# Attention split by engine and interleaved over both streams, with four modulation bursts moved to the output projection

## What is computed

```python
sm, cm, gm, sf, cf, gf = modulation(c, mod_w[l], mod_b[l])        # silu(c) @ w_mod, 2048 x 12288
h = rms_norm(x, norm_mix_pre[l]) * (1 + cm) + sm
q_a, k_a, v_a, q_b, k_b, v_b, u_c, v_c = split_projection(h, w_in[l])   # 2048 x 4608; gelu on u_c, v_c
o_a = neighbourhood_attention(...)    # 6 heads; context stream: plain attention
o_b = window_attention(...)           # 6 heads on 2 key heads, rotary, sink logit
o_c = chunk_gmlp(u_c, v_c, ...)       # layer norm, 128 x 128 mixing, gating
x = x + gm * rms_norm(merge_heads(o_a, o_b, o_c, w_out[l]), norm_mix_post[l])   # 2048 x 2048
x = ffn_sublayer(x, sf, cf, gf, ...)  # 5632 wide SwiGLU
```

## Time and profile before

| | us |
|---|---|
| median of 3 runs (2419.17 to 2423.46) | 2419.4 |
| the profiled execution | 2421.94 |
| its span | 2420.2 |
| TensorE busy | 2294.1 |
| VectorE busy | 1624.5 |
| ScalarE busy | 994.1 |

### The profile page before, as it was taken

The page is one execution under the profiler, slowest core; times in us unless marked ns, Lnnn a source line. Parts: engine busy times, 40 slices in busy tenths (PEclk is TensorE's granted clock), DMA queues, the critical chain, the costliest instruction groups (busy, mean ns, idle before and its releaser), DMA issues.

```text
span 2420.2 us, 27975 instructions
## 1 busy us (share of the span) xinstructions
PE 2294.1 (95%) x10686; PEld 1804.9 (75%) x10686; DVE 1624.5 (67%) x1738; ACT 994.1 (41%) x1284; POOL 68.9 (3%) x97
## 2 busy tenths in 40 slices
PE   5999878999999999999999998799999999999998
PEld 2776545778878888788777886487888888878886
DVE  2555443469988889888887996446888644454455
ACT  2333232364444444334346344346444444433443
POOL 1000010000000000000000101000000000000000
PEclk8999988999999999999999999899999999999999
DMA  8779888858878878788875897665877666656664
GB/s 305 271 278 340 331 291 304 297 178 296 285 258 291 289 264 295 249 275 286 287 244 204 306 316 245 230 184 169 278 269 254 211 195 190 186 178 195 190 219 148
DMA packets 269317, 609.91 MB, mean 252 GB/s; under 512 B 19116, under 2 KB 19296, under 8 KB 267840
## 3 DMA queue, kind: packets, MB, share of 16 engines
q1 hardware_dynamic: 264832, 589.37, 71.8%
q0 software_dynamic: 4352, 18.76, 2.1%
HBM read 603.79 MB, written 5.45 MB: 252 GB/s over the span
## 4 chain that ended last, share of the span: by engine, by line
PE 84%; DMA 7%; DVE 5%; issue 2%; ACT 2%; POOL 1%; SPq 0%; POOLq 0%; DVEq 0%; ACTq 0%
PE bank_A L849 39%; PE bank_B L849 38%; DMA mraw<-in_mod_w 6%; PE bank_M L909 2%; PE bank_X L937 2%; DVE wlo L1448 1%; PE bank_M L898 1%; ACT whi L1157 1%; PE bank_T L929 1%; DMA raw<-in_w_in 0%; DMA raw<-in_w_gate 0%; ACT junk L1171 0%; PE bank_M L838 0%; DVE xt_lo L1497 0%; POOL rstd L707 0%
## 5 line engine op out<-in xcount | busy, mean ns | idle before, releaser
L1448 DVE TENSOR_TENSOR wlo<-raw,whi 128x1024 fp32r<-128x1024 f32 x724 | 880.1, 1222 | 611.1 <-ACT whi L1157 610.5
L1157 ACT CAST whi<-raw 128x1024 fp32r<-128x1024 f32 x724 | 758.9, 1050 | 1178.0 <-PE bank_A L849 579.3
L849 PE MATMUL bank_B<-whi,xt_lo 128*128 128x512 f32 x1104 | 433.3, 392 | 1.1 <-DVE wlo L1448 0.6
L849 PE MATMUL bank_A<-whi,xt_lo 128*128 128x512 f32 x1088 | 429.6, 395 | 4.2 <-DVE xt_lo L1497 3.7
L849 PE MATMUL bank_B<-wlo,xt_hi 128*128 128x512 f32 x1104 | 429.9, 389 | 0.0
L849 PE MATMUL bank_B<-whi,xt_hi 128*128 128x512 f32 x1104 | 429.7, 389 | 0.0
L849 PE MATMUL bank_A<-wlo,xt_hi 128*128 128x512 f32 x1088 | 426.0, 392 | 0.0
L849 PE MATMUL bank_A<-whi,xt_hi 128*128 128x512 f32 x1088 | 425.7, 391 | 0.0
L1469 DVE SCALAR_TENSOR_TENSOR acc<-mraw,cond,acc 128x1024 f32<-128x1024 f32 x300 | 371.0, 1278 | 0.0
L849 PEld LDWEIGHTS bank_A<-whi,xt_lo 128*128 128x128 f32 x1088 | 205.9, 189 | 64.0 <-issue 19.8
L849 PEld LDWEIGHTS bank_B<-whi,xt_lo 128*128 128x128 f32 x1104 | 207.2, 188 | 54.9 <-issue 11.9
(11 more groups left out here) (231 smaller groups left out, 1623.6 us busy)
## 6 DMA issues: line engine op xcount, KB each, us to landing
mraw<-in_mod_w SPq DMA_DIRECT2D x384, 512.0 KB, 5.6
raw<-in_w_gate SPq DMA_DIRECT2D x176, 512.0 KB, 4.4
raw<-in_w_up SPq DMA_DIRECT2D x176, 512.0 KB, 4.4
raw<-in_w_down SPq DMA_DIRECT2D x176, 512.0 KB, 4.9
raw<-in_w_in SPq DMA_DIRECT2D x144, 512.0 KB, 5.4
raw<-in_w_out SPq DMA_DIRECT2D x64, 512.0 KB, 4.8
gate_mix<-gate_rows POOLq DMA_DIRECT2D x4, 1024.0 KB, 6.8
gate_ffn<-gate_rows POOLq DMA_DIRECT2D x4, 1024.0 KB, 9.4
```

The source lines that it names most:

```text
L849: mm = pe.matmul(bank[f"{pair}{s}"][:], xs[:, k, t], w[:, kb, :], start=(k == first and n == 0), stop=(k == (nk - 1 if last is None else l ...
L1157: act.copy(weights(u * UNIT + ph)[0], raw[:, ph % RING]).then_inc(hi_ready, 1)
L1448: dve.tensor_tensor(lo, raw[:, ph % RING], hi.bitcast(F32), ALU.subtract).then_inc(lo_ready, 1)
```

## The change

- The step list is the same for both layers and finer: `score` is cut into `score` (PE), `top` (DVE) and `exp` (ACT); `value` into `turn_p`, `mix` and `keep`; `gate_c` into `gate_c` and `lift`; `turn_c` into `turn_c` and `keep_c`. The steps of both streams and groups are interleaved. Waiting for z is a step of PE (`z`), both gelus stand near the front, the cached keys are transposed before the first score.
- Seven bursts stay in each attention. The second half of their last chunk goes behind piece 2 of the projection in both layers; layer 0's projection also has bursts behind pieces 5, 8, 11, 13, 16, 19, 21 and 24. SP issues their weights behind pieces 3 and 4 later in SP's own order. Tails go with them (`OUT_ENDS`).
- `ln_b` is kept in `junk` instead of a part of `pt`. POOL does its two powers for the layer norm ahead of `gate_store`. The output projection waits for each part of its input where it reads it first.

```diff
-MOD_OUT = [ND // 2, 0]
+MOD_OUT = [ND, 0]
...
+OUT_MODS = [{2: (-1, range(4, 8))}, {2: (-1, range(4, 8))}]
+OUT_MODS[0].update({q: (h // 2, range(4 * (h % 2), 4 * (h % 2) + 4)) for h, q in enumerate((5, 8, 11, 13, 16, 19, 21, 24))})
+OUT_FETCH = [{q + 3 + h: (mi, js[2 * h:2 * h + 2]) for q, (mi, js) in mods.items() if mi >= 0 for h in range(2)}
+             for mods in OUT_MODS]
+OUT_ENDS = [{2: -1, 24: ND - 1}, {2: -1}]
...
+def attention_steps():
...
+    first, second = ("mod_first",), ("mod_second",)
+    s = [first, ("z",), ("gelu", 0), ("turn", 0, 1), ("turn", 0, 3), ("turn", 0, 0), ("turn", 0, 2), ("turn", 0, 4), ("gelu", 1)]
+    s += [("turn_ck", 0), ("turn_ck", 1), ("score", 0), second, ("top", 0), ("exp", 0), ("bias",), ("sinks",), ("turn", 1, 2)]
+    s += [("turn_ws",), ("score", 1), ("top", 1), ("turn", 1, 4), ("turn", 1, 1), ("turn", 1, 3), ("exp", 1), ("soft", 0)]
+    s += [("turn", 1, 0), ("turn_p", 0), first, ("soft", 1), ("mix", 0), ("norm_v", 0), ("keep", 0), ("turn_p", 1)]
+    s += [("score", 2), ("top", 2), second, ("mix", 1), ("keep", 1), ("exp", 2), ("score", 3), ("top", 3), ("soft", 2)]
+    s += [("gate_c", 0), ("exp", 3), ("gate",), first, ("lift", 0), ("turn_p", 2), ("mix", 2), ("norm_v", 1), ("soft", 3)]
+    s += [second, ("turn_p", 3), ("turn_c", 0), ("keep", 2), ("keep_c", 0), ("gate_c", 1), ("mix", 3), ("lift", 1)]
+    s += [("turn_c", 1), first, ("keep", 3), ("keep_c", 1)]
+    return s
...
-        crossed, ln_b = pt[:, 0:8, :], pt[:, 8:12, :].rearrange("p t c -> p (t c)")
+        crossed, ln_b = pt[:, 0:8, :], junk[:]
...
                     if step[0] == "mod_first":
-                        mod_chunk(m_att, l, range(UNIT // 2 if l == 0 and m_att == m - 1 else UNIT))
+                        mod_chunk(m_att, l)
...
-                gate_store(l, 0)
                 for s in range(2):
                     power(vmv[:, s, 1:2], vrstd[:, s:s + 1], vmv_ready, 2 * l + s + 1, vrstd_ready)
+                gate_store(l, 0)
...
-                for step, banks in got.items():
-                    if step[0] in ("value", "turn_c"):
-                        for b, i in banks[-2:]:
-                            read(b, i)
+                mixed = {0: [("mix", 0), ("mix", 2)], NH: [("mix", 1), ("mix", 3)], 2 * NH: [("turn_c", 0), ("turn_c", 1)]}
...
+                        if i == 0 and k in mixed:
+                            for step in mixed[k]:
+                                for b, n in got[step]:
+                                    read(b, n)
...
+                    for j in range(UNIT - (i == ND - 1)):
+                        ahead(split, u + i, j, 1)
+                        if i * UNIT + j in OUT_ENDS[l]:
+                            mod_row(m + OUT_ENDS[l][i * UNIT + j])
```

More of the change, by code:

```diff
@@ L166, in mod_ends @@
+BANKS_OF = {"top": "score", "exp": "score", "keep": "mix", "lift": "gate_c", "keep_c": "turn_c"}
 def mod_ends(m):
@@ L287, in attention @@
                 banks = [self.turn()]
+            elif step[0] == "turn_p":
+                banks = [self.turn() for _ in range(2 if step[1] < 2 else 3)]
             elif step[0] == "score":
                 banks = [self.acc() for _ in score_banks(step[1])]
-            elif step[0] == "value":
-                banks = [self.turn() for _ in range(2 if step[1] < 2 else 3)] + [self.acc() for _ in range(2)]
+            elif step[0] == "mix":
+                banks = [self.acc() for _ in range(2)]
             elif step[0] == "gate_c":
@@ L1019, in attention @@
                             mm.then_inc(filled[b], 1)
-                    elif kind == "value":
+                    elif kind == "turn_p":
+                        n = step[1]
+                        pe.wait_ge(pn_ready, 4 * l + n + 1)
+                        blocks = [prob[:, n % 2, h, w * P:(w + 1) * P] for h in range(NH) for w in range(1 + n // 2)]
+                        for j, (b, i) in enumerate(banks):
+                            turn(b, i, blocks[4 * j:4 * j + 4])
+                    elif kind == "mix":
                         n = step[1]
                         s, ty = divmod(n, 2)
[L1023 to L1028, removed]
+                        for b, i in got[("turn_p", n)]:
                             read(b, i)
-                        for (b, i), heads in zip(outs, (range(0, 4), range(4, 6))):
+                        for (b, i), heads in zip(banks, (range(0, 4), range(4, 6))):
                             free(b, i)
@@ L1300, in attention @@
                     kind = step[0]
-                    if step in GELU_BEFORE:
-                        s = GELU_BEFORE.index(step)
+                    if kind == "gelu":
+                        s = step[1]
                         act.activation(z[:, s, U_C:W_IN], z[:, s, U_C:W_IN], ACT.Gelu_apprx_tanh).then_inc(gelu_ready, 1)
-                    if kind == "mod_second" and m < plan.at[(l, "out")][1] + MOD_OUT[l] - 1:
-                        mod_row(m)
                     elif kind in ("turn", "turn_ck", "turn_ws"):
@@ L1762, in attention @@
                         dve.tensor_tensor(v, v, ln_b, ALU.add).then_inc(vn_ready, 1)
-                    elif kind == "gate_c":
+                    elif kind == "lift":
                         s = step[1]
@@ L1772, in attention @@
                         ins.then_inc(freed[b], 1)
-                    elif kind == "turn_c":
+                    elif kind == "keep_c":
                         s = step[1]
```

125 lines of the change are left out of this document (49 added, 76 removed).

## The result

The changed kernel takes 2396.8 us (median of 4 executions, 2389.3 to 2398.6) against 2420.1 (4 executions, 2419.2 to 2423.5): 0.989 of the time, 95% interval 0.988 to 0.991, which is 23 us less. Two more sets of four gave 2390.4 and 2391.5 (first experiment). The direction and the range held; the three medians lie 10 to 17 us above the 2380 forecast.

The account below looks back on a forecast made before the run. TensorE, 95% busy, bounds the kernel; its attention waits come from the mraw ring (layer 0) and mainly the softmax chain (layer 1). -23.1 - 28.5 + 7.6 + 3 + 1.9 = -39.1 us from 2419.4 gives 2380; 80% between 2366 and 2402.

Parts of the forecast that it names:

- Attention, layer 1: Layer 1's attention stage: each turn costs a turn of the mraw ring, -23.1 us, bounds -28 and -15.
- the walk: Hand walk through layer 1's new attention list, each engine in order: mraw ring ends last, stage end moves 1572.4 to 1549.3.
- B: Rival for both attention stages: the softmax chain paces them, layer 1 saves 11.4 us, layer 0 25; 2395 us, chance 0.18.
- Attention, layer 0: Layer 0's attention stage: seven bursts paced by the mraw ring end at 380.5, not 408.98; -28.5 us, bounds -34 and -20.
- part (5): ln_b to junk, GpSimd's powers ahead of gate_store, gates behind the last score: costed at nothing, covered by the first output chunk.
- Output projection, layer 0: Layer 0's output projection: four more bursts cost +7.6 us, DMA stalls at two short gaps +3, bounds 0 and 12.
- wrong altogether: Sign of failure: attention over 75 us in either layer, or more than 12 us of waits in the projection.
- the turn of 6.2 us: Layer 0's quickest mraw turn, set against two-piece gaps of 5.44 us in its projection; 1.5 us stall taken for each.
- A: The forecast for both attention stages: the mraw ring paces them, 7 turns each; 2380 us, chance 0.50.
- Rival C: Layer 0's projection starves: weights arrive at 330 GB/s, +12 us for +3, 2389 us; at 283 GB/s 2405; chance 0.15.
- Output projection, layer 1: Layer 1's output projection: one more burst without DMA pressure, +1.9 us, bounds 1.8 and 3.
- My 377 GB/s over 85 us: Layer 0's projection: 61 transfers, 32 MB, pass on average at this rate in 84.9 us, with +3 us of stalls.

Follow-up runs that it names:

- first experiment: The changed kernel repeated without an edit, as the yardstick for the others: 2390.4 us, ratio 0.9865, in its first repeat and 2391.5 us, ratio 0.9875, in its second.
- Experiment 4: Against the changed kernel, modulation pieces that SP asks for in attention were fetched by half, 256 KB, with the same matmuls and waits: 2376.4 us, ratio 0.9806.
- experiment 3: The old order of steps, with seven bursts in each attention and the changed kernel's projections: 2423.8 us, ratio 1.0013 against the kernel before.
- experiment 7: The even kernel with the gate's rows loaded earlier, so that their 2 MB travel inside attention: 2391.8 us, ratio 0.9866.
- even kernel: The changed kernel with all nine bursts of layer 0's output projection three pieces apart, behind pieces 1, 4, 7, ... 25: 2381.4 us, ratio 0.9834, and 2381.0, ratio 0.9843.

## Why the prediction was right in direction and 10 to 17 us short

**Attention, layer 1: right, by its mechanism.** Predicted -23.1, measured -24.6. Experiment 4 shows that the ring held the stage and not the softmax chain, but the lead is smaller than in the walk: the first, third and sixth of the six turns ended by the chain of work, where the walk had that for the first, with a tie at the fifth. So B's mark came for half of the turns, but not its price of 11.4 us saved: with half pieces the new order goes through the stage in 51.6 us, where the old order with seven bursts takes 75.0 (experiment 3). From the first burst's end (1483.1) to the seventh's (1538.7) are 55.6 us; the walk had 57.0. That the sum came so near is partly luck, since two sizes were off and nearly cancel: the turn beside the stores took 11.5 us for 9 (its leg 9.76), the one where I had the gate's rows 8.3 for 12.

**Attention, layer 0: right mechanism, somewhat more.** Predicted -28.5 with an outer bound of -34, measured -35.0. The 12 us turn beside the gate's rows didn't come (8.6 us from 367.1 to 375.7), and the turn of 9.8 beside the stores was 8.4. Here part (5) failed: I put the rows' transfer in the last turn of attention and costed their new place at nothing, with the first output chunk as cover for their *use*. Their *bytes* have no such cover. They are not among the 61 transfers of my sum for the projection, and they met the first `w_out` pieces (10.37 us leg), the splits, and with them a tail that waits 1.3 us for VectorE in layer 0 and 1.5 in layer 1. Whether the projection pays for them is not shown: its first two bursts wait 0.75 and 1.7 us, but experiment 7, which sends the rows earlier, left it at 117.4 us, between the even kernel's two. Beside the ring the turn there is 12.2 and 13.5 us.

**Output projection, layer 0: the failed step.** Predicted +7.6 for four bursts and +3 of stalls; measured +25.4. The floor is as predicted: four bursts at 1.92 and a tail of 0.8 are 8.5. The other 16.9 us, against a bound of 12 in the prediction, are 12.0 of waits (the two rows of waits above) and 4.9 of matmuls that ran longer, at the lower clock shown below (busy time grew by 13.4 us, from 100.3 to 113.7, of which 8.5 are the floor). My own sign for "wrong altogether", more than 12 us of waits in the projection, was reached or passed in two of the three profiles of this kernel: 12.0, 12.7 in the first repeat and 9.8 in the second. The step that was wrong is the turn of 6.2 us, taken from attention's quickest leg of 4.59, at the two gaps of two pieces. The chain at the first of them:

```profile
421.93 1.06 ACT whi L1155
...
423.01 1.24 DVE wlo L1444
424.25 0.74 SPq L560
...
425.04 0.47 SPq L554
...
425.55 8.79 DMA mraw<-in_mod_w
...
434.48 1.93 PE bank_M L906 x8
```

The burst behind piece 11 ends at 423.6. SP, in its own order, first asks for a `w_out` piece (424.25), which must wait for the split of 423.01, and only then for the last piece of modulation weights (425.04); that one is 8.79 us under way between `w_out` traffic, and the burst behind piece 13 ends at 436.41. The turn is 12.7 us where the products and the burst itself cover 7.4. Its second like, and what follows either:

```profile
436.41 6.21 PE bank_B L846 x24
...
459.20 9.06 DMA mraw<-in_mod_w
...
470.32 6.34 PE bank_A L846 x24
```

The two gaps cost 5.2 and 4.6 us rather than 1.5 each (7.1 and 6.5 from the end of the products to that of the burst, less 1.92; 1 us of it is the second half of a burst at the lower clock), and the two pieces behind them took 6.21 and 6.34 rather than 5.44. The gaps of three pieces cost little once the queue is in step, 1.7 us behind piece 5 and 0.75 behind piece 2. Experiment 5, in which the two short gaps are gone, brought 9.0 and 10.4 us back, about what the two gaps cost. That the bursts are also spread over two more pieces there was not separated.

**Luck in the sum.** Layer 0's attention (-35.0, bound -34) and its projection (+25.4, where the bounds gave at most +19.6) both lay outside what I had allowed, in opposite directions. They cancel in part, and as far as that goes the nearness of the total is luck. The total by itself would even have pointed at B, which had 2395: only the stage times tell A from B.

**Rival C came nearer in size, not in kind.** At 330 GB/s it gave 2389, and the sets measured 2390 to 2397. But its mark was a DMA share of 1.0 throughout; the changed kernel has 0.86 at 309 GB/s, with stretches of idle queues between the stalls. The limit it names appears in the even kernel, whose windows stand below.

**The lower clock was not in the sum at all.** In the term for layer 0's projection I took every matmul behind the start at full speed, because the earlier trace rows show 0.98 where TensorE never waits. With waits in it that doesn't hold. Ten-us windows of the changed kernel (columns as in the earlier trace rows):

```profile
425.00:435.00 10.00, 5.92 (x32) 3.68 (x34) 2.45 (x2) 2.09 (x2) 0.00 (x0) 0.96 0.93 347
435.00:445.00 10.00, 10.00 (x44) 7.12 (x36) 2.43 (x3) 3.30 (x6) 0.00 (x0) 0.87 0.94 351
445.00:455.00 10.00, 10.00 (x52) 6.91 (x51) 4.69 (x6) 3.21 (x4) 0.00 (x0) 1.00 0.78 271
...
465.00:475.00 10.00, 6.61 (x26) 4.11 (x27) 1.23 (x1) 2.01 (x2) 0.00 (x0) 0.83 1.03 407
475.00:485.00 10.00, 10.00 (x57) 7.01 (x56) 4.97 (x5) 4.73 (x9) 0.00 (x0) 1.00 0.69 234
```

The window of its first repeat with the lowest clock:

```profile
440.00:450.00 10.00, 7.46 (x25) 4.74 (x26) 1.23 (x1) 1.33 (x2) 0.00 (x0) 0.66 1.03 409
```

Windows of the even kernel's second profile:

```profile
375.30:385.00 9.70, 7.11 (x40) 4.78 (x40) 0.00 (x0) 0.00 (x0) 0.00 (x0) 1.00 1.01 411
385.00:395.00 10.00, 9.97 (x52) 7.50 (x44) 4.99 (x5) 4.68 (x5) 0.00 (x0) 1.00 1.04 414
395.00:405.00 10.00, 10.00 (x53) 6.89 (x51) 3.40 (x4) 3.14 (x3) 0.00 (x0) 1.00 1.01 361
...
425.00:435.00 10.00, 9.59 (x50) 6.33 (x49) 3.67 (x3) 2.29 (x4) 0.00 (x0) 1.00 0.99 343
435.00:445.00 10.00, 9.02 (x47) 5.81 (x46) 3.99 (x5) 4.36 (x7) 0.00 (x0) 1.00 0.99 348
```

In the changed kernel the windows that hold the end of a long wait, or the one after it, show a granted clock of 0.83 to 0.96; in the first repeat one shows 0.66, so the larger part of it ran at 1.2 of the 2.4 GHz. In the even kernel's second profile, with at most 1.4 us waited at once, all ten-us windows of the stage stand at 1.00; in its first, the window behind waits of 2.9 and 1.3 us shows 0.70. The length of a wait alone doesn't decide it: in the second repeat of the changed kernel, waits of 0.9 and 1.4 us at the start of the stage went with this window:

```profile
385.00:395.00 10.00, 8.11 (x35) 5.91 (x36) 5.00 (x5) 4.58 (x5) 0.00 (x0) 0.83 0.79 260
```

**Output projection, layer 1: right**, +2.2 for +1.9.

**Rates.** The Trainium skill (DMA: Bandwidth & Descriptors, section Where 436 GB/s comes from) has about 358 GB/s per core as the HBM's side. Here ten-us windows of the even kernel's projection start reach 411 and 414 GB/s; five in a row behind them, from 395 to 445 us, carry 340 to 361 with a DMA share of 0.99 to 1.01. As a ceiling the trace goes above it; as a rate held over 50 us beside both kinds of transfer it is close. My 377 GB/s over 85 us were not held by any of these kernels.

**Left open.** The start of the span, which the change doesn't touch, varied from 315.5 to 320.4 us between profiles; and the changed kernel's own spread of 15 us goes with its clock without my knowing what sets the one execution apart from the other. How far the fixed part of a turn could be cut was not tried.

## What to carry to other kernels

When two limits stand close behind one another (here a ring of transfers and a chain of steps), cost each part of a change against the other limit: the order alone gave 16 us, the moved bursts nothing, both together 23 to 29. Work that is moved beside full transfers must be spaced by the turn of its own ring as it is *there*, not as it was at its quickest: here equal gaps of three pieces beat a mixture of three and two by 9 to 10 us. And a wait on TensorE costs more than its length, since what follows may run at half the clock.

## What the runs showed of the hardware that I had not expected

- A 2 MB turn through four 512 KB places took 8.4 us on the mean in layer 0's new attention, 11.5 beside the stores in layer 1's, 12.2 and 13.5 beside the gate's rows (experiment 7), and 11.5 to 12.9 at the two short gaps of the projection over the three profiles of the changed kernel. Its last leg alone was 4.59 us at its quickest in the trace of before, 6.1 to 7.0 in most turns of the new attention (9.76 beside the stores), and 8.8 to 9.9 in the projection of the first profile.
- In one stage of the even kernel the DMA engines read as fully busy (0.99 to 1.01) both at 411 GB/s and at 340 to 361. What makes the difference was not tested.
- Waits of 3 to 4 us among dense products went with a granted clock of 0.66 to 0.87 in a ten-us window at or behind their end. Waits of up to 1.4 us left 1.00 in the second set of the even kernel, but went with 0.83 at the start of one projection of the changed kernel.
